# Output projection and feed-forward part as one block, with the first token half prepared inside the projection

## What is computed

```python
o = jnp.concatenate([_rmsnorm(o_sb, sb_out_gain), _rmsnorm(o_dsa, dsa_out_gain)], axis=-1)
x = x + g1[:, None, :] * (o @ w_o)
h = _modulate(_rmsnorm(x, norm2_gain[l]), sh2, sc2)      # h * (1 + sc2) + sh2
x = x + g2[:, None, :] * ((silu(h @ w_gate) * (h @ w_up)) @ w_down)
sh_f, sc_f = jnp.split(c_act @ w_mod_final + b_mod_final, 2, axis=-1)
return _modulate(_rmsnorm(x, final_gain), sh_f, sc_f)
```

## Time and profile before

| | us |
|---|---|
| median of 3 runs | 1523.64 |
| runs, from and to | 1521.10 to 1524.06 |
| profiled execution, its own time | 1525.2 |
| span of the profile | 1523.5 |
| TensorE busy in it | 1333.1 (88%) |
| VectorE busy | 1074.5 (71%) |
| ScalarE busy | 733.0 (48%) |
| POOL busy | 761.2 (50%) |

### The profile page before, as it was taken

One profiled execution on the slowest core, in us unless ns is written; L12 is line 12 of the kernel. 1 busy time (PEld: TensorE's weight loads), 2 busy tenths in 40 slices (PEclk: granted clock), 3 DMA queues, 4 the chain that ended last, 5 costly groups with the idle time before them and its releaser, 6 DMA issues. The chain is left out here.

```text
span 1523.5 us, 18602 instructions
## 1 busy us (share of the span) xinstructions
PE 1333.1 (88%) x6085; PEld 1079.4 (71%) x6085; DVE 1074.5 (71%) x1565; ACT 733.0 (48%) x1263; POOL 761.2 (50%) x686
## 2 busy tenths in 40 slices
PE   2779999994777788886899579999999999999997
PEld 2657888784656666664677457888888888888786
DVE  4848589997777776764366877666666666577787
ACT  4436577734777777775312533333333333354332
POOL 1163444554445438888100266555555556586552
PEclk9989899996898899998799889999999999999999
DMA  9670234355243233320533514444444445889532
GB/s 336 183 207 18 70 121 153 127 180 145 56 111 74 51 97 97 84 70 28 207 105 117 207 55 159 159 159 159 159 160 159 159 159 188 304 305 338 172 116 111
DMA packets 124396, 223.35 MB, mean 147 GB/s; under 512 B 9451, under 2 KB 52565, under 8 KB 124053
## 3 DMA queue, kind: packets, MB, share of 16 engines
q1 hardware_dynamic: 124308, 222.27, 44.7%
HBM read 160.90 MB, written 57.93 MB: 144 GB/s over the span
## 5 line engine op out<-in xcount | busy, mean ns | idle before, releaser
L1964 POOL TENSOR_TENSOR dn_lo<-dn_raw,dn_hi 128x512 fp32r<-128x512 f32 x77 | 127.4, 1672 | 66.6 <-ACT dn_hi L1852 66.6
L1821 ACT ACTIVATE wgu_hi<-wgu_sum 128x512 fp32r<-128x512 f32 x88 | 55.5, 632 | 205.8 <-DVE wgu_sum L2165 77.5
L2062 PE MATMUL ps_ffn<-h_t_hi,wgu_hi 128*128 128x512 f32 x352 | 137.9, 392 | 10.2 <-DVE wgu_lo L2180 10.2
L1945 POOL TENSOR_TENSOR wgu_lo<-wgu_raw,wgu_hi 128x512 fp32r<-128x512 f32 x66 | 94.7, 1442 | 102.0 <-ACT wgu_hi L1821 102.0
L2062 PE MATMUL ps_ffn<-h_t_lo,wgu_hi 128*128 128x512 f32 x352 | 137.6, 391 | 0.0
L2062 PE MATMUL ps_ffn<-h_t_hi,wgu_lo 128*128 128x512 f32 x352 | 137.4, 390 | 0.0
L1852 ACT ACTIVATE dn_hi<-dn_raw 128x1024 fp32r<-128x1024 f32 x77 | 81.3, 1062 | 114.4 <-PE ps_ffn L2086 58.8
L1140 POOL TENSOR_TENSOR a_rows<-beta,stick_left 128x1024 f32<-128x1024 f32 (+3 forms) x64 | 77.1, 1206 | 109.0 <-DVE stick_left L1186 108.9
L413 POOL TENSOR_TENSOR win_lo<-win_raw,win_hi 128x256 fp32r<-128x256 f32 (+1 forms) x84 | 62.8, 777 | 137.1 <-ACT win_hi L404 137.1
L2086 PE MATMUL ps_ffn<-dn_hi 128*128 128x512 f32 x308 | 120.2, 390 | 0.0
L2086 PE MATMUL ps_ffn<-dn_hi,dn_lo 128*128 128x512 f32 x308 | 119.8, 389 | 0.0
(11 more groups left out here) (309 smaller groups left out, 3696.6 us busy)
## 6 DMA issues: line engine op xcount, KB each, us to landing
scr_act_sums<-act_sums SPq DMA_DIRECT2D x11, 1792.0 KB, 6.9
dn_raw<-scr_act_sums SPq DMA_DIRECT2D x77, 256.0 KB, 5.3
wgu_raw<-in_w_gate_dram SPq DMA_DIRECT2D x11, 1024.0 KB, 5.4
wgu_raw<-in_w_up_dram SPq DMA_DIRECT2D x11, 1024.0 KB, 5.4
wd_sums<-in_w_down_dram SPq DMA_DIRECT2D x11, 1024.0 KB, 5.0
scr_wd_sums<-wd_sums SPq DMA_DIRECT2D x11, 1024.0 KB, 4.1
dn_raw<-scr_wd_sums SPq DMA_DIRECT2D x44, 256.0 KB, 7.0
win_raw<-in_w_in_dram SPq DMA_DIRECT2D x20, 512.0 KB, 4.4
```

The source lines that it names most:

```text
L1821: act.activation(sh[slot(m, x)][:], src, ACT.Copy).then_inc(whi, 1)
L1945: pool.tensor_tensor(sl[slot(m, x)][:], src, sh[slot(m, x)][:].bitcast(F32), ALU.subtract).then_inc(wlp, 1)
L1964: pool.tensor_tensor(bl[q % NSLOT][:, 1], braw[:, entry(q), 1], bh[q % NSLOT][:, 1].bitcast(F32), ALU.subtract).then_inc(dlw, 1)
L2062: last = pe.matmul(bank(m, b), a[s][:, t], h[x][t // 2][:, t % 2], start=(fresh and t == 0 and a is sh and h is hh), stop=(t == 3 and a is ...
```

## The change

Both phases share one block without a barrier between them, one set of 8 PSUM banks and one plan of SBUF; each hands its parts of the engines' programs over, and some of phase5's run inside phase4's loops. The 32 final steps are all put behind tiles 0 to 7, four to a tile. VectorE scales x1 blocks 0 to 3 in place behind tile 8, once they are spilled; TensorE transposes them (bank 7, one group at a time) between the matmuls of tiles 9 to 13; ScalarE modulates behind its copies of tiles 11 to 15; VectorE does three of the four first splits behind tiles 10 to 12. x1 is spilled block by block during the projection. The first weight loads go out when y_sb(15) is done. The gates and the second modulation vector are made earlier. POOL makes the rstd of blocks 4 and 5, of 6 and of 7 in three pieces, with the first weight subtractions between them. Buffers lie at other places in SBUF; the slots of the first down steps are freed by other products than before.

```diff
+    NF, FY = 4 * KD, 8
+    STEP_T = {(0, 9): 0, (1, 10): 1, (0, 10): 2, (1, 11): 3, (0, 11): 4, (1, 12): 5, (0, 12): 6, (0, 13): 7}
+    AFTER_COPY = {11: (0, 1), 12: (2, 3), 13: (4, 5), 14: (6,), 15: (7,)}
+    def final_steps(n):
+        return range(NF * n // FY, NF * (n + 1) // FY) if n < FY else ()
...
     def sync(sp):
+        for n in range(NY):
+            for f in final_steps(n):
+                load_final(f)
...
+            if n == NY - LEAD - 1:
+                then.first_raw(sp)
+            if n % 2:
+                then.spill(sp, n // 2)
...
     def scalar(act):
-                    if n % 2 == 0 and n >= 4:
-                        squares(n // 2 - 2)
+            if n % 2 and n >= 3:
+                squares((n - 3) // 2)
+            for t in AFTER_COPY.get(n, ()):
+                then.modulate(act, t)
+        then.first_highs(act)
...
     def gpsimd(pool):
+        late_rstd(4, 6, 2)
+        then.first_lows(pool, 0)
+        late_rstd(6, 7, 3)
+        then.first_lows(pool, 1)
+        late_rstd(7, 8, 4)
+        then.first_lows(pool, 2)
...
     def tensor(pe):
             if n + LEAD < NY:
                 y_sb(n + LEAD)
+            if (1, n) in STEP_T:
+                then.transposes(pe, STEP_T[1, n])
             y_d(n)
+            if (0, n) in STEP_T:
+                then.transposes(pe, STEP_T[0, n])
...
     def vector(dve):
-                    if n < NY - 2:
-                        for f in range(NF * n // (NY - 2), NF * (n + 1) // (NY - 2)):
-                            final_step(f)
+            for f in final_steps(n):
+                final_step(f)
+            if n == 8:
+                for x in range(4):
+                    then.xhat(dve, x)
+            if n in (10, 11, 12):
+                then.split(dve, n - 10)
...
+    def transposes(pe, n):
+        h, t = n // KD, n % KD
+        pe.wait_ge(xhd, 4 + 4 * h)
+        if h:
+            pe.wait_ge(hfr, max(KD, n - 3))
+            pe.wait_ge(p4.yfr, p4.NY)
+            pe.wait_ge(p4.ysc, p4.NY)
+        elif n:
+            pe.wait_ge(hfr, n)
...
+    def xhat(dve, i):
+        dve.wait_ge(p4.rs2, (1, 2, 3, 4)[max(0, i // 2 - 1) + (i == 7)])
+        if i < 4:
+            dve.wait_ge(x1_out[0], 16 * 4)
+            dst = g.x1[:, i]
...
-            for i in range(3):
-                xhat(i)
-            xhat(4)
-            xhat(5)
-            split(P_A11, f_t2, 0, 2, 1)
-            split(P_A11, f_t2, 1, 4, 2)
-            xhat(6)
-            xhat(7)
+        for i in range(4, 7):
+            xhat(dve, i)
             w_sum(0, P_S1)
+        xhat(dve, 7)
             w_sum(1, P_S1)
-            split(P_A12, f_t4, 0, 6, 3)
-            split(P_A12, f_t4, 1, 8, 4)
+        split(dve, P_A12, f_t4, 1, 8, 4)
```

More of the change, by code:

```diff
@@ new lines, in phase4 @@
+    wh = sbuf(nc, ctx, "wo_hi", [P, KD, D], F32R)
+    with ExitStack() as c:
+        wl_d = sbuf(nc, c, "wo_lo_d", [P, NPAIR, D], F32R)
+    wr_d = sbuf(nc, ctx, "wo_raw_d", [P, NPAIR, D])
+    g1 = sbuf(nc, ctx, "gate1", [P, D])
+    us = sbuf(nc, ctx, "y_sb", [P, 2, HALF])
+    hf = sbuf(nc, ctx, "y_full", [P, 2, HALF])
+    yg = sbuf(nc, ctx, "y_gated", [P, 2, HALF])
+    rc = sbuf(nc, ctx, "rstd_col", [P, 2 * NT])
+    mb = sbuf(nc, ctx, "mb2", [P, 2 * KD])
+    fa = sbuf(nc, ctx, "mod_acc_final", [P, HALF])
@@ new lines, in phase5 @@
+    xh = [low("xhat_45", [P, 2, D], 16), low("xhat_67", [P, 2, D], 24)]
+    wslot = lambda x: 4 * x if x < 4 else 48 + 4 * (x - 4)
+    sh = [low(f"wgu_hi{x}", [P, 4, P], wslot(x), F32R) for x in range(NPOS)]
+    sl = [low(f"wgu_lo{x}", [P, 4, P], wslot(x) + 2, F32R) for x in range(NPOS)]
+    sf = [low(f"wgu_sum{x}", [P, 4, P], wslot(x) + 2) for x in range(NPOS)]
+    raw = [high(f"wgu_raw{x}", [P, KD, 2 * P], 104 - 8 * x) for x in range(2)]
+    u2, p1 = (high(name, [P, 2, HALF], kb) for name, kb in (("u2_part", 56), ("p1_part", 52)))
@@ L1605, in phase5 @@
+    u4 = low("u4_part", [P, 2, HALF], 60)
     acts = over_x1("act_sums", [P, 8, HALF], 0)
@@ new lines, in w_lo_pool @@
+    def w_lo_pool(pool, m, x):
+        q = J.at[m, x]
+        pool.wait_ge(whi, q + 1)
+        src = sf[slot(m, x)][:] if x in SUMS else part(m, x)
+        if x == P_S3 or x == P_S4:
+            pool.wait_ge(sums, sums_through(m, x))
+        pool.tensor_tensor(sl[slot(m, x)][:], src, sh[slot(m, x)][:].bitcast(F32), ALU.subtract).then_inc(wlp, 1)
+    def transposes(pe, n):
+        h, t = n // KD, n % KD
+        pe.wait_ge(xhd, 4 + 4 * h)
[5 more added lines that the diff above has]
+            pe.wait_ge(hfr, n)
+        for b in range(4):
+            src = xh[b // 2][:, b % 2, P * t:P * t + P] if h else g.x1[:, b, P * t:P * t + P]
+            m = pe.transpose(ps[:, tbank(n), P * b:P * b + P], src, g.ident[:])
+        m.then_inc(tr, 1)
@@ new lines, in first_highs, with first_lows, early_split @@
+    def first_highs(act):
+        for x in (P_A11, P_A12):
+            for m in range(2):
+                w_hi(act, m, x)
+    def first_lows(pool, part):
+        for m, x in (((0, P_A11), (1, P_A11)), ((0, P_A12),), ((1, P_A12),))[part]:
+            w_lo_pool(pool, m, x)
+    def early_split(dve, n):
+        split(dve, (P_A11, P_A12)[n // 2], (f_t2, f_t4)[n // 2], n % 2, 2 * n + 2, n + 1)
+    then.first_raw, then.spill, then.modulate, then.first_highs = first_raw, spill, modulate, first_highs
@@ L2414 @@
+    then.first_lows, then.transposes, then.xhat, then.split = first_lows, transposes, xhat, early_split
+    return Programs(sync, scalar, gpsimd, tensor, vector)
 class Names:
```

1746 lines of the change are left out of this document (868 added, 878 removed).

## The result

The changed kernel took 1549.20 us (median of 4 runs, 1544.9 to 1553.3) beside 1522.37 us for the kernel before on the same chip (1521.06 to 1524.06): **1.0171 times, 95% interval 1.0148 to 1.0194, 26.8 us slower**. The forecast had the sign and less than half the size (12.2 us), and 1549 lies outside its range. The profiled execution has a span of 1551.1 us; its `y_full` of tile 0 comes at 762.30, 3.0 us later than before's. That is no part of the change's price: it comes from the clock at the head of the projection, shown under what stays open.

The account below looks back on a forecast made before the run. VectorE's list behind the seam was taken to set when TensorE's dense run starts. Projection 23.7 us later, less 11.1 and 1.4 won back, plus 1 for spills, gave 12.2 us on 1523.64, so 1536; range 1528 to 1547.

Parts of the forecast that it names:

- Final steps in the first 8 tiles: Projection: four steps a tile wait on load turnarounds and stores, making tile 8's `y_full` 23.4 us later, at 829.8.
- The wait for the scaled tiles: Projection: TensorE idles about 16 us before its first transposes, then loses 3 us at the lower clock.
- The last x1 tile: End of the projection: finished at 869.1 against 845.44, 23.7 us later, with ScalarE's modulations costed at nothing.
- From there to VectorE's sum: Last x1 tile to VectorE's sum for S2: 9.5 us in place of 20.6, so 11.1 us won back.
- The two waits for POOL's rstd: After the last x1 tile: VectorE waits twice, as rstd 6 comes 3.0 and rstd 7 5.8 us behind it.
- On to the dense run, "1.4 won back": VectorE's sum to the dense run: 28.9 us less a 1.39 us wait for TensorE; second-half modulations bounded at 0 to 1.5.
- The sum of these, 12.2: Whole kernel: 23.7 - 11.1 - 1.4 + 1 = 12.2 us later.
- Moved buffers ... lie under the dense run: nothing.: Dense run: moved buffers and later slot release cost nothing, as data is there some 10 us ahead.
- The spills, 1 us: SyncE's queue: four 512 KB stores of x1 among the final loads cost a quarter of a us each.
- The final steps did not keep up with the tiles (1508): Rival, projection: load turnaround fits a tile, TensorE never waits, 1508; chance 0.06, its middle form (1524) 0.04.
- The final loads get slower: Rival, projection: spills and x1 traffic delay loads 1.5 us each, plus longer half clock, giving 1545; chance 0.14.
- the early half isn't early: Rival, projection: TensorE stops for scaling at tile 9, transposes cost more than they hide; counted within the forecast, no own chance.

Follow-up runs that it names:

- e4: The kernel before with four final steps behind each of tiles 0 to 7 and nothing else changed; 1534.0 us, 1.0064 times the kernel before.
- e3: The changed kernel with 32 bytes of padding at the top of SBUF, so all tiles start on multiples of 64 bytes; 1549.0 us, 1.0167 times before.
- e7: The changed kernel with top-counted tiles 32 bytes lower and bottom-counted ones 128 higher, so both operands' starts agree; 1541.3 us, 1.0099 times before.
- e1: The kernel before with the token tiles of the feed-forward products 32 bytes higher and everything above 112 KB 64 higher; 1535.8 us, 1.0066 times before.
- e2: The kernel before with the weight tiles and what lies above them 32 bytes higher; 1535.9 us, 1.0076 times before.
- e6: The kernel before with the weight tiles and what lies above them 128 bytes higher; 1536.1 us, 1.0081 times before.
- e5: The kernel before with every tile of the feed-forward part 32 bytes higher; 1523.1 us, 0.9986 times before.
- e11: The kernel before with the weight tiles 256 bytes higher; 1525.3 us, 0.9999 times before.
- e8: e7 with the final steps spread over 14 tiles in place of 8; 1532.1 us, 1.0050 times the kernel before.
- e14: e8 with the final steps dealt so that those waiting for a store (8, 16, 24) come first in a tile; 1523.1 us, 1.0001 times before.

## Why the forecast was right and wrong

- **Final steps in the first 8 tiles.** Tile 8's `y_full` was forecast 70.5 us behind tile 0's and came 71.2 behind. Right, by the mechanism named: pairs of loads and the store. As a price it needs e4 beside it: by itself this lateness costs the kernel only 8 to 10 us.
- **The wait for the scaled tiles.** 16 us forecast, 15.73 measured, then a lower clock for a while. Right. TensorE's window behind the wait (granted clock in the third column from the right):

```profile
838.00:850.00 12.00, 11.41 (x44) 0.73 0.11 44
```

A granted clock of 0.73 over 12 us is a loss of 3.2 us (an estimate from this row); the forecast took 3.

- **The last x1 tile.** It ended at 874.93, 112.6 behind the first `y_full` (e3 113.2, e7 113.0); forecast 109.8. Of the 2.8 us missing, 1.1 are a wait for a modulation (the last row of the list of waits), which I had costed at nothing with "some 1 us a group" as the price of that cover gone, and 1.1 a `y_gated` of 1.78 us where others take 0.69.
- **From there to VectorE's sum.** 9.5 us forecast, 7.7 measured (874.93 to 882.62). The two waits for POOL's rstd, the sign that the forecast named, are not there: VectorE has no idle time in this stretch, and the last power ends at 878.37, 3.4 us behind the last x1 tile where the forecast had 5.8.

```profile
877.43 0.94 POOL L1442 TENSOR_TENSOR rstd<-rstd,nhalf 128x1 f32<-128x1 f32 x1
```

- **On to the dense run, "1.4 won back".** Forecast 27.5 us, measured 28.2 (882.62 to 910.85), and 29.2 in e3 and in e7. The 1.4 was the wait in front of 879.34, which the other five traces of the old order don't have: they take 27.5 us as they are. What the forecast had only as a bound of 0 to 1.5 us came instead: VectorE waits for the second half's modulations (`h_sum_b`), 0.42 us in the changed kernel, 1.4 in e3 and e7. So nothing was won here and 0.7 to 1.7 us lost.
- **The sum of these, 12.2.** On this pair of traces the errors cancel: 2.8 and 0.7 more, 1.8 less, and the 1 us for the spills that no trace shows apart make 12.9. Against the usual trace of the old order the price is some 15. The mechanism is in the main the one forecast; that the first pair came within 1 us was luck.
- **"Moved buffers ... lie under the dense run: nothing."** This is the step that failed: a term put at nothing that measured 11.7 us. I had asked of the new places only whether data would be there in time, and taken a TensorE that never waits for one that runs at a fixed pace. e1, e2, e6 (slower pace) against e5, e11 (the old one) show that the pace hangs on where the two operands start against each other, and e7 and e8 give the 11 us back in the changed kernel itself. That term alone takes the forecast from 1536 to 1548. The forecast's own rows held two paces without a remark: it counted 5.60 us for 24 matmuls in the projection, 0.233 each, while the dense run of the kernel before makes one in 0.226.
- **The spills, 1 us.** Not told apart by any run.
- **The rivals.** The final steps did not keep up with the tiles (1508). "The final loads get slower" (1545) is nearest in number, but not what happened: tile 8 came within 1 us of the forecast. The fourth rival, "the early half isn't early", was passed over as counted. It was worth more than that: e8 shows 6.7 us of it with the bunching gone, by the wait for a store. It ended on the same side, so nothing in the chances hung on it.

What stays open: the first `y_full` comes at 754.8 to 765.3 us in the 16 traces, with no order that the edits explain (after 762.3, before 759.3, e7 765.0, e14 755.0). Part of the medians' scatter of 2 to 3 us between kernels whose A and B agree will come from there. Up to 3.4 us of it is TensorE's clock. From the projection's first matmul to the first `y_full` it is 28.8 us in the kernel before, 32.1 in the changed one, and 32.1 as well in e1, e2, e6 and e11, which have the old order. The window from 752 to 759 shows it (count, granted clock, DMA share, GB/s), before and then after:

```profile
752.00:759.00 7.00, 7.00 (x38) 1.00 0.00 1
```

```profile
752.00:759.00 7.00, 7.00 (x24) 0.52 0.00 0
```

TensorE is busy throughout in both; in the changed kernel's trace the clock is at its lower level (1.2 GHz) for nearly all of it. What decides it was not looked for.

## What to carry to other kernels

When tiles are moved, compare the starts of the two operands of each hot matmul modulo 256 bytes, and after the change count the matmuls in a window of the dense run: busy share, waits and clock were all perfect here while each product took 3% longer. A wait for a store or a load in an engine's list is priced by what stands behind it: the waits of 4 to 6 us for a store cost some 2 us in one order of work and 6 to 8 in another, and dealing the steps so that the waiting one comes first in the next tile took most of it away. The longest of them, in tile 3, cost next to nothing. Lateness in the middle of a stage is not lateness at its end: over 20 us at tile 8 were worth 8 to 10. And a forecast that agrees with one pair of traces isn't yet confirmed: set the trace of before beside others of its kind.

## What the runs showed of the hardware

- Products of 128x128 by 128x512 (four-byte operands, full granted clock) follow each other every 0.2264 to 0.2265 us when all token tiles and weight tiles of the stage start at the same remainder of 256 bytes (before, e5, e11: 1568, 1567, 1568 in 355 us), and every 0.233 when none of the token tiles does (e1, e2, e6: 1523, 1523, 1524). At 2.4 GHz the difference of 0.0067 us is some 16 cycles. Distances of 0 and 256 bytes were free, 32 and 128 cost the same; 64 and 192 were not tried. The absolute start doesn't matter (e5: both 32 bytes past a multiple of 64).
- Where a kernel mixes agreeing and other products, the cost isn't proportional: 230.3 and 234.4 ns in the changed kernel, as said above. In e3, where a part of the token tiles agrees with the weights and the others lie 128 bytes off, the count (1531) is between the two.
- The projection of the kernel before runs at the slower pace, 5.60 us for 24 matmuls of the same shape, 0.233 each. Whether the starts of its operands are the cause no run tried. If they are, its 384 matmuls would give some 2.6 us (an estimate from the 0.0067 us).
- The Trainium skill (TensorE: Matmul & The Clock Gate, Step-by-step: what each phase is for) says of the engine's two read ports that loading the next tile's weights "doesn't steal SBUF read bandwidth from the running matmul", and gives a gap of 215.7 ns for 512 columns. The gap measured here is 226.4 ns at best, with a weight load for each product and four-byte operands. On the ports no run here decides: nothing but addresses was moved, and the pace went from 226.4 to 233. That the weight load and the moving operand meet in the same part of SBUF is my guess at the cause, and no run shows it.
- The Trainium skill's page SBUF — State Buffer (Operand start alignment) asks for starts at multiples of the element size and calls that legality, not speed. Every start tried here obeys it, and the speed still depends on the start.
